# A block of key products moved under the condition's weight loads

## The reference, cut to what matters

```python
mod = silu(c) @ w_ada + b_ada                 # one row of 3 x 1024: shift, scale, gate
h = rms_norm(x, norm_g) * (1.0 + scale) + shift
... = split(h @ w_in, IN_OFFSETS)             # inputs of four branches: retention (d), stick breaking (c), banded (b), sparse (a)
merged = sum_i sigmoid(h @ w_merge[i]) * ((y_i * silu(z_i)) @ w_br[i])
x = x + gate * (merged @ w_out)
# second block, for layer i in (0, 1): convolution (0) or differential attention (1), then
k = (mem @ mem_w_k[i]); v = (mem @ mem_w_v[i])       # mem: 256 tokens of 1024, the same for both layers
x = x + softmax(rms(x) @ mem_w_q[i] . k) v @ mem_w_o[i]
x = x + swiglu(rms(x))
```

## Time and profile before

| | |
|---|---|
| median of three runs | 1202.02 us (1199.81 to 1203.36) |
| profiled execution | 1202.58 us, its span 1201.3 us |
| granted TensorE clock, mean | 0.987 of full |
| VectorE, ScalarE, POOL busy | 749.3, 589.8, 58.6 us |
| moved by DMA | 198.82 MB, mean 166 GB/s |
| narrow products of H with a weight | 3 x 1080, 284 to 286 ns each as recorded |
| VectorE's low parts | 184, 404.4 us |

### The profile page before, as it was taken

How to read it: one execution, slowest core, us unless ns; L and a number is a source line. 1 busy time by engine, 2 the same in 40 slices (tenths; PEclk the granted TensorE clock), 3 DMA queues, 4 the chain that set the end, 5 groups by cost and what they waited for, 6 DMA issues and landing times.

```text
span 1201.3 us, 16688 instructions
## 1 busy us (share of the span) xinstructions
PE 1154.2 (96%) x7018; PEld 1025.8 (85%) x7018; DVE 749.3 (62%) x938; ACT 589.8 (49%) x800; POOL 58.6 (5%) x80
## 2 busy tenths in 40 slices
PE   5999999999998998999999999999899999999997
PEld 3799888788888987898999998787787988999986
DVE  4944766565676997664666555555667656555543
ACT  5545754344563672554535443445565455444432
POOL 2020100000000000000200000000003001000000
PEclk9999999899998999999999999999899999999999
DMA  9874543365555402443554655565226534455550
GB/s 341 291 249 121 182 142 122 96 232 197 185 170 182 170 1 73 173 158 109 177 176 141 210 194 173 188 216 193 74 103 199 180 116 152 162 192 176 176 193 36
DMA packets 106604, 198.82 MB, mean 166 GB/s; under 512 B 5985, under 2 KB 22465, under 8 KB 106528
## 3 DMA queue, kind: packets, MB, share of 16 engines
q1 hardware_dynamic: 102976, 186.46, 46.5%
q0 software_dynamic: 3552, 11.29, 3.0%
HBM read 196.69 MB, written 1.05 MB: 165 GB/s over the span
## 4 chain that ended last, share of the span: by engine, by line
PE 74%; DVE 14%; ACT 7%; issue 2%; POOL 2%; DMA 1%; SPq 0%; DVEq 0%; ACTq 0%; POOLq 0%
PE product L545 66%; DVE conv_out L2319 4%; DVE w_low L501 3%; ACT w_high L492 3%; DMA w_raw<-in_w_ada 1%; PE small L578 1%; PE small L1790 1%; PE small L1173 1%; ACT drows L2672 1%; PE small L1184 1%; DVE drows L2752 1%; DVE stats L2754 1%; PE small L1811 1%; DVE drows L2767 0%; POOL stats L658 0%
## 5 line engine op out<-in xcount | busy, mean ns | idle before, releaser
L501 DVE TENSOR_TENSOR w_low<-w_raw,w_high 128x2048 fp32r<-128x2048 f32 (+3 forms) x184 | 404.4, 2203 | 247.1 <-ACT w_high L492 244.9
L492 ACT ACTIVATE w_high<-w_raw 128x2048 fp32r<-128x2048 f32 (+3 forms) x184 | 338.0, 1841 | 191.6 <-PE product L545 160.3
L545 PE MATMUL product<-H_low,w_high 128*128 128x256 f32 x1080 | 308.5, 286 | 6.9 <-DVE w_low L501 6.0
L545 PE MATMUL product<-H_high,w_high 128*128 128x256 f32 x1080 | 307.3, 285 | 0.0
L545 PE MATMUL product<-H_high,w_low 128*128 128x256 f32 x1080 | 306.7, 284 | 0.0
L545 PEld LDWEIGHTS product<-H_low,w_high 128*128 128x128 f32 x1080 | 208.0, 193 | 9.3 <-DVE w_low L501 6.3
L545 PEld LDWEIGHTS product<-H_high,w_low 128*128 128x128 f32 x1080 | 208.1, 193 | 0.3
L545 PEld LDWEIGHTS product<-H_high,w_high 128*128 128x128 f32 x1080 | 208.0, 193 | 0.0
L545 PE MATMUL product<-w_high,H_low 128*128 128x512 f32 (+2 forms) x384 | 150.4, 392 | 0.0
L545 PE MATMUL product<-w_high,H_high 128*128 128x512 f32 (+2 forms) x384 | 149.0, 388 | 0.0
L545 PE MATMUL product<-w_low,H_high 128*128 128x512 f32 (+2 forms) x384 | 148.4, 387 | 0.0
(11 more groups left out here) (366 smaller groups left out, 1564.6 us busy)
## 6 DMA issues: line engine op xcount, KB each, us to landing
w_raw<-in_ffn_w_gate SPq DMA_DIRECT2D x20, 1024.0 KB, 5.1
w_raw<-in_ffn_w_up SPq DMA_DIRECT2D x20, 1024.0 KB, 5.2
w_raw<-in_ffn_w_down SPq DMA_DIRECT2D x20, 1024.0 KB, 5.1
w_raw<-in_w_merge SPq DMA_DIRECT2D x16, 1024.0 KB, 5.0
w_raw<-in_w_ada SPq DMA_DIRECT2D x12, 1024.0 KB, 6.9
w_raw<-in_w_in SPq DMA_DIRECT2D x8, 1024.0 KB, 5.6
w_raw<-in_mem_w_k SPq DMA_DIRECT2D x8, 1024.0 KB, 5.0
w_raw<-in_conv_w_pw SPq DMA_DIRECT2D x16, 512.0 KB, 4.5
```

Of the source, the lines that this page charges most:

```text
L492: k.act.eng.activation(chunk_view(k, k.w_high[j], i), chunk_view(k, k.w_raw[i % k.N_RAW], i), ACT.Copy).then_inc(*k.act.tells("weights_hig ...
L501: k.vec.eng.tensor_tensor(low, raw, high.bitcast(F32), ALU.subtract).then_inc(*k.vec.tells("weights_low", ("weights low", i)))
L545: mm = pe.eng.matmul(bank[:, off:off + wide], a, r, start=b not in started, stop=True, skip_group_check=True)
```

## The change

1. The plan begins with layer 0's key weights, 512 columns as four half pieces and 512 as two pieces, between the pieces of scale and shift. The four gate pieces come between the first branch steps' weights. The key weights around w_out are now layer 1's, and the differential attention has no key steps.
2. TensorE starts with the transposes of the memory, the first keys (six steps), and x's transposes. The keys are copied to HN, stored to DRAM (`key_store`), and later loaded into `mem_keys`, layer 0's in the convolution stage and layer 1's at the start of the differential attention.
3. The condition's product is gone from TensorE: pieces of `w_ada` aren't split; VectorE multiplies each of their four 128-row parts with one number of silu(c) per partition and adds it up (`vec_modulate`), and TensorE sums over the partitions, with a column of ones for scale and shift, with all ones for the gate.
4. The first norm is applied by feature: x is scaled by its root by token on ScalarE, transposed, and VectorE multiplies and adds per-partition columns.

```diff
+    halves = [chunks(keys[0], KT, [(c, S)]) for c in range(0, CN, S)]
+    second, first_in = chunks(keys[0], KT, [(CN, CN)]), chunks(w_in, KT, [(W_D_Q, 512)])
+    plan.extend(halves[c][f] for f in range(KT // CK) for c in range(CN // S))
+    plan.extend(modulation(ada, "scale", 0) + modulation(ada, "shift", 0) + second[:1] + modulation(ada, "scale", 1) + second[1:])
+    shift = modulation(ada, "shift", 1)
+    plan.extend([shift[0], first_in[0], shift[1], first_in[1]])
+    add(w_in, [(W_D_V, 512)])
+    gate = modulation(ada, "gate", 0) + modulation(ada, "gate", 1)
+    for block in ((W_C_Q, 512), (W_C_V, 512), (W_B_Q, 384), (W_B_V, 384)):
+        add(w_in, [block])
+        plan.append(gate.pop(0))
...
-    add(w["mem_w_k_2"][0], [(0, CN)])
+    add(keys[1], [(0, CN)])
     square(w["w_out"][0])
-    add(w["mem_w_k_2"][0], [(CN, CN)])
+    add(keys[1], [(CN, CN)])
...
+def vec_modulate(k, i):
+
+    V, (name, c, first) = k.vec, k.plan[i][2]
+    raw, total = chunk_view(k, k.w_raw[i % k.N_RAW], i), k.sums_of[name][:, c:c + CN]
+    V.wait_ge("c silu", ("weights", i))
+    for j in range(CK):
+        number = k.c_silu[:, first + j:first + j + 1]
+        V.wait_ge(V.last, "gate bias" if name == "gate" else None)
+        if first + j == 0 and name != "gate":
+            V.eng.tensor_scalar(total, raw[:, j, :], number, None, ALU.mult).then_inc(*V.tells("modulations", (name, c // CN)))
+        else:
+            V.eng.scalar_tensor_tensor(total, raw[:, j, :], number, total, ALU.mult, ALU.add).then_inc(
+                *V.tells("modulations", (name, c // CN), ("weights low", i)))
...
+def pe_modulations(k, n):
+
+    bank = k.small.take(("columns", n))
+    k.pe.wait_ge(("scale", n), ("shift", n), k.small.before(("columns", n)))
+    for i, name in enumerate(("scale", "shift")):
+        for j in range(CK):
+            c = (CK * n + j) * P
+            mm = k.pe.eng.matmul(bank[:, CK * i + j:CK * i + j + 1], k.sums_of[name][:, c:c + P], k.ones[:, 0:1], start=i == 0 and j == 0, stop=True,
+                                 skip_group_check=True)
+    mm.then_inc(*k.pe.tells("columns", ("columns", n)))
...
+    pe.wait_ge("common", "c row", "condition rows")
+    bank = k.small.take("condition")
+    pe.eng.transpose(bank[:, 0:4 * KT], k.cond_rows[:, :], k.ident[0:4 * KT, 0:4 * KT]).then_inc(*pe.tells("turned", "condition turned"))
+    for g in range(0, KT, CK):
+        for t in range(NT):
+            pe_turn(k, ("first mem", g, t), k.first_mem[:, t, :], [P * (g + i) for i in range(CK)], "first mem")
+    drain(pe_first_keys(k, 0))
+    last = pe_first_keys(k, 1)
+    next(last)
+    pe_turn_x(k, 0)
+    pe_modulations(k, 0)
+    drain(last)
+    pe_turn_x(k, 1)
...
+    A.wait_ge("condition turned")
+    A.eng.activation(k.c_silu, k.small.of("condition")[:, 0:KT], ACT.Silu).then_inc(*A.tells("c_silu", "c silu"))
+    for g in range(0, KT, CK):
+        for t in range(NT):
+            act_turn(k, ("first mem", g, t), k.mem_first, g, t)
+        act_split(k, g // CK)
+    act_chunk(k)
+    act_chunk(k)
     sums = k.stat(("sums", "first"), NT)
-    for i in range(len(MODS)):
-        act_chunk(k)
-        act_chunk(k)
-        if i in (2, 4):
-            for t in range(NT):
-                act_turn(k, ("first", i // 2 - 1, t), k.H_first, (i // 2 - 1) * CK, t)
-        if i == 0:
-            for t in range(NT):
-                A.wait_ge(A.last, "x loaded")
-                A.eng.activation(k.HN[:, t, :], k.X[:, t, :], ACT.Square, accum_out=sums[:, t:t + 1]).then_inc(*A.tells("squares", "first squares"))
+    for t in range(NT):
+        A.wait_ge("x loaded")
+        A.eng.activation(k.scaled_x[:, t, :], k.X[:, t, :], ACT.Square, accum_out=sums[:, t:t + 1]).then_inc(*A.tells("squares", "first squares"))
+    keys(0, 0)
+    keys(0, 1)
+    for t in range(NT):
+        A.wait_ge(A.last, ("root", "first"))
+        A.eng.activation(k.scaled_x[:, t, :], k.X[:, t, :], ACT.Copy, scale=k.stat(("root", "first"), NT)[:, t:t + 1]).then_inc(*A.tells("scaled_x", "scaled x"))
+    act_chunk(k)
+    act_first_half(k, 0)
+    act_chunk(k)
+    act_chunk(k)
+    act_chunk(k)
+    keys(1, 0)
+    keys(1, 1)
+    act_first_half(k, 1)
...
+def vec_first_half(k, n):
+    V, columns, ps = k.vec, k.stat(("columns", n), 2 * CK), k.small.of(("columns", n))
+    at = slice(CK * n, CK * (n + 1))
+    gain, bias, scale = (k.cond_cols[:, ROWS[name]:ROWS[name] + KT][:, at] for name in ("norm_g", "shift", "scale"))
+    V.wait_ge(V.last, ("columns", n))
+    V.eng.tensor_tensor(columns[:, 0:CK], ps[:, 0:CK], scale, ALU.add).then_inc(*V.tells("vec_steps"))
+    V.eng.tensor_tensor(columns[:, CK:2 * CK], ps[:, CK:2 * CK], bias, ALU.add).then_inc(*V.tells("vec_steps", k.small.free(("columns", n))))
+    V.wait_ge(V.last)
+    V.eng.scalar_tensor_tensor(columns[:, 0:CK], columns[:, 0:CK], 1.0, gain, ALU.add, ALU.mult).then_inc(*V.tells("columns_copied", ("columns copied", n)))
+    for b in range(2):
+        for j in range(2):
+            f = 2 * b + j
+            V.wait_ge(V.last, ("x turned", n, b))
+            V.eng.tensor_scalar(k.whole[:, f, :], k.small.of(("x", n, b))[:, S * j:S * (j + 1)], columns[:, f:f + 1], columns[:, CK + f:CK + f + 1],
+                                ALU.mult, ALU.add).then_inc(*V.tells("whole", ("whole", n, b), k.small.free(("x", n, b))))
+    for b in range(2):
+        at = slice(CK * n + 2 * b, CK * n + 2 * b + 2)
+        V.wait_ge(("first high", n, b))
+        V.eng.tensor_tensor(k.H_first.low[:, at, :], k.whole[:, 2 * b:2 * b + 2, :], k.H_first.high[:, at, :].bitcast(F32), ALU.subtract).then_inc(
+            *V.tells("operand_low", k.H_first.ready(n)))
...
+    V.wait_ge("condition turned", "c silu")
+    V.eng.tensor_copy(k.cond_cols[:, KT:4 * KT], k.small.of("condition")[:, KT:4 * KT]).then_inc(*V.tells("cond_cols", k.small.free("condition")))
+    for g in range(0, KT, CK):
+        for t in range(NT):
+            vec_turn(k, ("first mem", g, t), k.mem_first, g, t)
+        vec_split(k, g // CK)
+    for _ in range(3):
         vec_chunk(k)
+    vec_first_half(k, 0)
+    vec_chunk(k)
+    vec_chunk(k)
+    vec_first_half(k, 1)
+    vec_chunk(k)
...
+        yield from pe_block(k, "d_qk", k.H_first, KT, FEATURES, inside={(0, 40): lambda: pe_modulations(k, 1)})
...
     g.eng.dma_start(k.tap_rows[:, :], k.w["conv_w_dw_2"][0]).then_inc(*k.landed("load_taps", "tap rows"))
+    g.wait_ge("second keys")
+    g.eng.dma_start(k.key_store[1], k.mem_keys[:, :, :].rearrange("p k n -> p (k n)")).then_inc(*k.landed("store_keys", ("keys stored", 1)))
+    g.wait_ge(("keys stored", 1))
+    pool_load_keys(k, 0)
     g.wait_ge("conv gains free")
     pool_row(k, "gain1", k.gains[1][:, :], k.w["conv_b_pw2_2"][0], "conv b2")
...
     k.norms["after", 0].pool_finish()
+    pool_load_keys(k, 1)
...
-        for i, _ in enumerate(pe_memory_keys(k, 1)):
+        for i, _ in enumerate(pe_memory_values(k, 1)):
...
+        if into == ("shift", 0, 0):
+            sp.eng.dma_start(k.X[:, :, :], w["x"][0].rearrange("(t p) n -> p t n", p=P)).then_inc(*k.landed("load_x", "x loaded"))
```

More of the change, by code:

```diff
@@ L158, in weight_plan @@
     even(w["diff_w_q_2"][0])
-    memory(1)
+    even(w["mem_w_v_2"][1])
     square(w["diff_w_o_2"][0])
@@ L531, in pe_block @@
         pe.chunk += 1
-        high, low = (chunk_view(k, t[i % k.N_SPLIT], i) for t in (k.w_high, k.w_low))
-        pe.wait_ge(("weights low", i), x.ready(first // CK))
+        high, low = (chunk_view(k, t[i % k.N_SPLIT], k.split[i]) for t in (k.w_high, k.w_low))
+        pe.wait_ge(("weights low", k.split[i]), x.ready(first // CK))
         n = 0
@@ L964, in act_merge_gate @@
     slot = k.sig.take(key)
-    A.wait_ge(k.sig.before(key))
+    A.wait_ge(k.sig.before(key), ("keys stored", 0))
     for step in range(2):
@@ L1502, in mem @@
     def mem():
+        for n in range(D // CN):
+            bank = k.small.take(("gate sums", n))
+            k.pe.wait_ge(("gate", n), k.small.before(("gate sums", n)))
+            k.pe.eng.matmul(bank[:, :], k.ones, k.gate[:, n * CN:(n + 1) * CN], start=True, stop=True).then_inc(*k.pe.tells("columns", ("gate sums", n)))
+        yield
         for t in range(NT):
@@ L1584, in mem @@
     def mem():
+        for n in range(D // CN):
+            V.wait_ge(("gate sums", n))
+            V.eng.tensor_scalar(k.gate[:, n * CN:(n + 1) * CN], k.small.of(("gate sums", n))[:, :], 0.25, None, ALU.mult).then_inc(
+                *V.tells("gate", "layer gate", k.small.free(("gate sums", n))))
+        yield
         for t in range(NT):
@@ L1748, in act_memory_keys, with act_memory_values @@
                                      k.product.of((key, b))[:, :].rearrange("p (k n) -> p k n", n=S), ACT.Copy).then_inc(
-                        *A.tells("memory_kv", ("mem keys", layer), k.product.free((key, b))))
+                        *A.tells("memory_kv", "second keys", k.product.free((key, b))))
             yield
+def act_memory_values(k, layer, behind=None):
```

(3 more changed lines are left out.)

159 lines of the change are left out of this document (79 added, 80 removed).

## The result

The changed kernel takes 1222.39 us (median of 4 runs, 1221.52 to 1223.43) against 1202.07 before (4 runs): ratio 1.0168, interval 1.0153 to 1.0184. That is slower, within the range of 1201 to 1225, 7.4 us above the forecast of 1215. Its profiled execution took 1223.43, 20.85 above the one of before.

A forecast was written before the change was run, and what follows sets the result against it. DMA bounds the kernel before 60 us, TensorE from 60 to 340, cross-engine chains in convolution and differential attention. Start +12.3, branches +1.0 and +2.1, convolution +3.3, attention -5.8 sum to +12.9: 1215 us, range 1201 to 1225.

The forecast's parts named there:

- Start, +12.3: Start until d_qk's second step ends: 82.7 instead of 70.4 us, with three TensorE waits; bounds +3.9 and +16.
- The clock's 6.0: Start: lower clock after each of three TensorE waits costs 2.0 us, 6.0 in all; bounds 0 and 7.5.
- the second key block's start at 35: Start: the second key block's piece lands at 30.5 us and, after its split, its first step can start at 35.
- Branches, +3.1: Branches: gate sums on VectorE mostly covered, +1.0 us; two gate sums on TensorE, +2.1, all on the path.
- the case named for a failed cover: Branches: a block of four gate sums (3.2 us) delays retention's or stick breaking's next step, at worst twice, 6 us.
- Convolution, +3.3: Convolution: bias-gains row, behind the keys' store (6.0 us), lands at 373.6 instead of 370.38, shifting everything; bounds 0 and +8.
- Attention, -5.8: Differential attention: rounds with a split keep their length; 5.8 of 23.8 us of key steps come off; bounds 0 and -23.8.
- the clock's 1 us: Differential attention's end: 1 us allowed for the lower clock in the output projection after the idle rounds.
- A: Start holds at its lower end without clock loss and the convolution's row is early: +1.5, 1203.5 us; chance 0.14.
- B: Differential attention: TensorE sets the rounds, so key steps come off in full, -23.8: total -5, 1197 us; chance 0.11.
- C: Much slower: keys' store and reload late +8, gate sums delay retention +5, start +16: +25, 1227 us; chance 0.13.
- D: Differential attention not shortened, since the second half's chain sets its end: 0 for -5.8, 1221 us; chance 0.12.

The follow-up runs named there:

- experiment 2: Changed kernel with 10, 6 and 4 extra products on TensorE at its waits before the second key block's steps and d_qk's second step: 1220.77 us.
- Experiment 5: Changed kernel with only one of the four sums of each gate piece left on VectorE, loads and TensorE's gate sums unchanged: 1218.21 us.
- 4: Changed kernel with start's splits before the input's halves, bias-gains row before the keys' store, gate pieces three and four moved to branch b's query weights: 1205.63 us.
- Experiment 6: Changed kernel with GpSimd's row of convolution bias gains issued ahead of the keys' store and load: 1218.16 us.
- experiments 3: Changed kernel with the last two gate pieces loaded and summed behind branch a's weights, not between branch b's: 1226.39 us.
- experiment 8: Changed kernel with four blocks of six extra products on TensorE in rounds of the differential attention: 1221.25 us.
- experiment 7: Kernel before with only the four key steps taken out of the differential attention, raw weights loaded in place of the keys: 1197.62 us.
- experiment 10: Version with splits and row first, gate earlier and all first keys before modulations, plus shift sums moved to TensorE as single-column products: 1217.60 us.

## Why the prediction was right, and where 7.4 us are missing

- **The view of the kernel.** Right. TensorE is the bound behind the start, and the start's 16.0 stand undiminished at 132 us, behind three of the gate's four blocks of sums (96.26, 109.29 and 127.96).
- **Start, +12.3.** Measured +16.0. The three waits came, 12.7, 7.7 and some 5.4 us long (9, 7 and 5 forecast), and behind them narrow products 0.21 apart, as in the earlier trace rows; wide products begin at 86.20, not at 80 to 85. The clock's 6.0 was right: 8.03 and 7.45 against 5.94, and 19.53 against 16.92, are 6.2 (the last of the three also by experiment 2). The step that failed is the second key block's start at 35: its piece landed at 33.84, not 30.5, and it began at 38.15; every later point of the schedule carries that 3.2. I had allowed 2.7 us for a load queue that runs dry, and it took 6: between 10 and 20 us DMA moved 263 GB/s, where it had moved 389. The reason named came true: SyncE waited 7.9 us for VectorE's first split, which ended at 13.77, and issued its next piece at 13.79. No run moves this term. Two of the bounds were added up wrongly: DMA never dry is 2.7 less by the same numbers, not 2.4, and the upper end's 12.3, 3 and 1.5 make 16.8, not 16; neither changes the forecast. The Trainium skill, "TensorE: Matmul & The Clock Gate", section "HAM oscillation — how this bites in real kernels", has an example in which each throttled tile loses half of 1.67 us; an estimate by it is 2.5 us for the three waits, and these traces show 6.2.
- **Branches, +3.1.** Measured +6.7, a miss of 3.6, as large as the start's 3.7 and of the same sign. The two gate sums cost 1.7 (2.1 forecast). VectorE's sums cost 5.0, not 1.0, and the case named for a failed cover (a block in front of stick breaking, up to 6) is what happened, with one block of the four: 2.5 us of wait and most of the rest as lower clock behind it. I judged the cover by VectorE's busy share over 229 us, 135.6 of 229.5. In the six microseconds of the kernel before in which that block was to stand, VectorE was busy for 6.06 of 6.39. In equally long stretches ahead of the three blocks that cost nothing it was busy for 4.59, 2.92 and 3.34 (74.0, 87.0 and 105.6 us in the kernel before; the second is shown below):

```profile
87.00:93.40 6.40, 6.40 (x52) 6.15 (x52) 2.92 (x3) 2.08 (x2) 1.53 (x3) 1.00 1.04 184
...
120.00:126.39 6.39, 6.39 (x44) 6.34 (x43) 6.06 (x10) 3.80 (x7) 2.57 (x2) 1.00 0.59 168
```

  Experiment 5 shows that the sums alone do it, and 4 that two pieces' distance avoids it.
- **Convolution, +3.3.** Measured +2.9 at the add and +3.4 behind the stage. The wait for the store took 6.04 (6.0 forecast). Experiment 6 confirms the row as the cause at the add. That the sum behind the stage fits to 0.1 is partly luck: in the taps the difference is 2.1, and 1.3 more comes at 491 to 496, where the granted clock was 0.77 in this execution and 1.00 at the same place in experiments 3 and 8.
- **Attention, -5.8.** Measured -4.7, and -4.8 alone in experiment 7. Rounds with a split in them kept their length with the key steps' products and without them (experiment 7), and extra products beside and behind the last split changed nothing (experiment 8). In the 35 us that answer to 890 to 925 TensorE was busy 23.91 us against 32.40, 8.5 less and not 12 to 20, at a mean clock of 0.66. The step that was mis-sized is the clock's 1 us: the projection's first step alone grew by 2.1 (13.14 against 11.06).
- **The rivals.** A falls with its start. B falls by experiment 7. C had the right sizes in two terms (start 16, branches 5), though not its larger convolution; its deciding point, the row later than 376, did not come: 395.97 less the 22.7 brought along from earlier is 373.3, against 373.6 forecast. D falls by the same run as B.

The sum of the changed terms, 16.0 + 6.7 + 3.4 - 4.7 = 21.4, is the 20.85 of the profiled executions to within 0.6. The measured time lies between the forecast and C's 1227: the mechanism held in all four parts, and the 7.4 us are the start's 3.7, the branches' 3.6 and the attention's 1.1, less about 1 for the rest.

## What to carry to other kernels

A busy share over a long stretch does not tell whether an engine has room; look at the few microseconds where the added block will stand, and at what is queued behind it. Where two engines release each other in turn, put the split for the next product ahead of the work that the product doesn't need: that alone was worth 10.7 us here, two thirds of what the start had lost. Work taken from an engine that does not set the pace gives back only what its leaving shortens on the chain, 4.8 of 23.8 us.

## What the hardware showed that I had not expected

- TensorE can be busy and still have the lower clock. In experiment 10, 32 products of one column followed each other without a gap, and the granted clock fell while they ran (0.98 of full from 38 to 40 us, 0.50 from 40 to 50; TensorE was busy 10.00 us of 10 and 9.36 of 10 in the stretches shown):

```profile
38.00:48.00 10.00, 10.00 (x57) 10.00 (x56) 0.00 (x0) 1.91 (x1) 0.00 (x0) 0.60 0.47 165
...
68.00:78.00 10.00, 9.36 (x44) 9.28 (x44) 2.08 (x5) 0.00 (x0) 0.00 (x0) 0.50 0.71 234
```

- One wait of 2.53 us cost 5.0: products of 384 columns came 0.32 apart behind it until 151.9, then 0.17.
- The same eight column sums took 1.70 us at the full clock and 3.56 at the lower one.
- The clock can dip in one execution and not in another at the same place, with TensorE busy in both. From 250 to 254 us TensorE was busy 4.00 of 4.00 us in the changed kernel and in experiment 6; the granted clock was 0.88 and 0.51, and experiment 6 lost 1.6 us there that its edit has no part in.
